# The modulation's product in a two-layer transformer kernel: split operands and four cheap products in place of one full-precision product

## What is computed

```python
# first block, layer 0: the NSA heads of the mixer (8 heads, 2 key groups, three branches)
pc = masked_softmax(q . kc)      # compressed keys: 31 columns
ps = masked_softmax(q . k_slc)   # selected keys, causal: up to 512 columns
pw = masked_softmax(q . k_win)   # window keys, causal: up to 512 columns
o  = g0 * pc @ vc + g1 * ps @ v_slc + g2 * pw @ v_win
# second block: the modulation, from two vectors c and c_ctx of 1024
sh1, sc1, g1, sh2, sc2, g2 = split(silu(c) @ ada_w + ada_b, 6)       # ada_w: 1024 x 6144
csh1, csc1, ...            = split(silu(c_ctx) @ ada_w + ada_b, 6)
```

## Time and profile before

| | |
|---|---|
| runs | 3551.23 us median of 3 (3548.71 to 3552.36) |
| the profiled execution | 3549.85 us, of which the span of the trace is 3548.4 us |
| PE busy | 3301.7 us, 93% |
| DVE busy | 2273.8 us, 64% |
| ACT busy | 1303.9 us, 37% |
| POOL busy | 807.3 us, 23% |
| granted TensorE clock, mean | 0.964 of full speed |

### The profile page before, as it was taken

One profiled execution on the slowest core, in us unless ns is written; L12 is line 12 of the kernel. 1 busy time (PEld: TensorE's weight loads), 2 busy tenths in 40 slices (PEclk: granted clock), 3 DMA queues, 4 the chain that ended last, 5 costly groups with the idle time before them and its releaser, 6 DMA issues. The chain is left out here.

```text
span 3548.4 us, 45109 instructions
## 1 busy us (share of the span) xinstructions
PE 3301.7 (93%) x17156; PEld 2753.9 (78%) x17156; DVE 2273.8 (64%) x4365; ACT 1303.9 (37%) x2284; POOL 807.3 (23%) x751
## 2 busy tenths in 40 slices
PE   7999989999999999997998998866889999999998
PEld 6445548888766688885776877766889999999998
DVE  4666445646455565464553336997778888888886
ACT  3333333223333332233453223225863333343433
POOL 1000341000100020004000002376853333334341
PEclk9999989999999999997998998988999999999999
DMA  3332102222211132222111222243579989899883
GB/s 136 125 108 76 51 24 89 95 102 87 93 48 42 42 107 91 100 89 69 65 35 57 90 89 83 85 159 129 211 274 316 323 309 321 308 319 316 308 313 124
DMA packets 180454, 515.17 MB, mean 145 GB/s; under 512 B 14992, under 2 KB 75408, under 8 KB 175120
## 3 DMA queue, kind: packets, MB, share of 16 engines
q1 hardware_dynamic: 128256, 305.70, 25.1%
q0 software_dynamic: 40464, 160.45, 13.2%
q10 hardware_dynamic: 11520, 46.15, 3.4%
HBM read 477.10 MB, written 35.13 MB: 144 GB/s over the span
## 5 line engine op out<-in xcount | busy, mean ns | idle before, releaser
L230 PE MATMUL bank<-h_hi,w_hi 128*128 128x512 f32 (+1 forms) x2528 | 970.4, 384 | 76.3 <-ACT w_hi L198 21.1
L230 PE MATMUL bank<-h_lo,w_hi 128*128 128x512 f32 (+1 forms) x2528 | 953.9, 377 | 0.0
L204 DVE TENSOR_TENSOR w_lo<-w_raw,w_hi 128x1024 fp32r<-128x1024 f32 (+1 forms) x468 | 599.8, 1282 | 333.5 <-ACT w_hi L198 327.6
L198 ACT ACTIVATE w_hi<-w_raw 128x1024 fp32r<-128x1024 f32 (+1 forms) x508 | 546.0, 1075 | 543.8 <-PE bank L230 526.3
L230 PEld LDWEIGHTS bank<-h_hi,w_hi 128*128 128x128 f32 x2528 | 487.9, 193 | 163.4 <-issue 48.5
L230 PE MATMUL bank<-h_hi,w_lo 128*128 128x512 f32 (+1 forms) x2528 | 596.7, 373 | 16.3 <-POOL w_lo L211 16.3
L230 PEld LDWEIGHTS bank<-h_lo,w_hi 128*128 128x128 f32 x2528 | 488.9, 193 | 67.4 <-issue 11.4
L230 PEld LDWEIGHTS bank<-h_hi,w_lo 128*128 128x128 f32 x2528 | 460.0, 189 | 86.1 <-POOL w_lo L211 17.6
L230 PE MATMUL bank<-e_hi,w_hi 128*128 128x384 f32 x1024 | 345.4, 337 | 5.9 <-DVE e_lo L2262 5.9
L230 PE MATMUL bank<-e_lo,w_hi 128*128 128x384 f32 x1024 | 344.2, 336 | 0.0
L2171 POOL DMA_INDIRECT own_row<-in_u_rows,own_e x128 | 157.9, 1233 | 321.5 <-DVE sums L2299 277.5
(11 more groups left out here) (405 smaller groups left out, 4754.1 us busy)
## 6 DMA issues: line engine op xcount, KB each, us to landing
w_raw<-in_w SPq DMA_DIRECT2D x476, 512.0 KB
ada_w<-in_ada_w POOLq DMA_DIRECT2D x24, 1024.0 KB, 5.1
expert_weights<-G ACTq DMA_DIRECT2D x12, 2048.0 KB, 7.3
Gin<-expert_weights SPq DMA_DIRECT2D x32, 768.0 KB
w_raw<-in_w SPq DMA_DIRECT2D x32, 704.0 KB
hidden_ahead<-u_stage ACTq DMA_DIRECT2D x40, 192.0 KB, 3.4
ahead<-hidden_ahead SPq DMA_DIRECT2D x20, 384.0 KB
na_bias<-in_bias ACTq DMA_DIRECT2D x4, 896.0 KB, 4.5
```

What stands on the lines that cost most here:

```text
L198: sc.activation(w_hi[s][:, 0:n], w_raw[raw_slot[u]][:, 0:n], ACT.Copy).then_inc(*w_hi_made.next(u))
L204: ve.tensor_tensor(w_lo[s][:, 0:n], w_raw[raw_slot[u]][:, 0:n], w_hi[s][:, 0:n], ALU.subtract).then_inc(*w_lo_made.next(u))
L230: m = te.matmul(out, wt, moving, start=(not low and k == 0 and moving is hi), stop=(low and k == len(blocks) - 1))
```

## The change

The modulation's product is taken apart as the large products are. DVE splits silu(c) once into a rounded part and a rest, side by side as `silu4` [128, 8, 4] of type fp32r. `ada_w` is loaded in halves of 512 KB into four buffers. For each half, ACT makes the rounded copy `ada_hi` (L807 of the new kernel) and POOL the rest `ada_lo` (L811); both lie in the tiles 0 to 3 of `o_hi` and `o_lo`, two buffers each. PE then does 4 matmuls with the four columns of `silu4` against `ada_hi` and 4 against `ada_lo` (L796, L799), where it did 4 fp32 matmuls with two columns. A row of the result is [4, 256], and the turn (L817) adds its two parts by a product with `fold` in place of the identity. ACT makes the copy for slot g+1 behind the exponentials of slot g; POOL makes the rest behind that, and then issues the load of four halves ahead. On PE the half product moves from ahead of the query matmuls and the value sums to behind them, to the end of the slot. The making of `fold` waits for the load of `ident`, one of the kernel's first.

```diff
-        ada_in = [loaded(f"ada_in{b}") for b in range(2)]
+        silu4 = sb(st, "silu_parts", [P, KT, 4], F32R)
+        fold = sb(st, "ada_fold", [4, 2])
+        ada_in = [loaded(f"ada_in{b}") for b in range(4)]
...
+        ada_hi, ada_lo = [[o[:, 2 * b:2 * b + 2, :].rearrange("p u (c n) -> p (u c) n", n=256) for b in range(2)] for o in (o_hi, o_lo)]
...
-            ve.tensor_tensor(silu[:, :, :], silu[:, :, :], col("c", 0, 16).rearrange("p (k c) -> p k c", c=2), ALU.mult).then_inc(*dve.next("silu"))
+            ve.tensor_tensor(silu[:, :, :], silu[:, :, :], col("c", 0, 16).rearrange("p (k c) -> p k c", c=2), ALU.mult).then_inc(*dve.next())
+            ve.wait_ge(*dve.here())
+            ve.tensor_copy(silu4[:, :, 0:2], silu[:, :, :]).then_inc(*dve.next())
+            ve.wait_ge(*dve.here())
+            ve.tensor_tensor(silu4[:, :, 2:4], silu[:, :, :], silu4[:, :, 0:2], ALU.subtract).then_inc(*dve.next())
+            ve.wait_ge(*ident_in.at("in"))
+            ve.tensor_tensor(fold[:, :], ident[0:4, 0:2], ident[0:4, 2:4], ALU.add).then_inc(*dve.next("silu"))
...
-            for c in range(4 * half, 4 * half + 4):
-                m = te.matmul(sums, silu[:, c, :], ada_w[k % 2][:, c, :], start=(c == 0), stop=(c == KT - 1))
+            te.wait_ge(*act.at("ada hi", g))
+            for c in range(4):
+                te.matmul(sums, silu4[:, 4 * half + c, :], ada_hi[g % 2][:, c, :], start=(half == 0 and c == 0), stop=False)
+            te.wait_ge(*pool.at("ada lo", g))
+            for c in range(4):
+                m = te.matmul(sums, silu4[:, 4 * half + c, :], ada_lo[g % 2][:, c, :], start=False, stop=(half == 1 and c == 3))
+            m.then_inc(*pe.next("ada", g))
+
+        def ada_scalar(g):
+            if g < slots:
+                sc.wait_ge(*ada_in[g % 4].at(g))
+                if g >= 2:
+                    sc.wait_ge(*pe.at("ada", g - 2))
+                sc.activation(ada_hi[g % 2], ada_w[g % 4][:, :, :], ACT.Copy).then_inc(*act.next("ada hi", g))
+
+        def ada_pool(g):
+            gp.wait_ge(*act.at("ada hi", g))
+            gp.tensor_tensor(ada_lo[g % 2], ada_w[g % 4][:, :, :], ada_hi[g % 2], ALU.subtract).then_inc(*pool.next("ada lo", g))
...
-                for n in range(2) if g == 1 else (g,) if 1 < g < slots else ():
-                    ada_tensor(n)
...
+                if g in (1, 2):
+                    ada_tensor(g - 1)
+                if g == 2:
+                    ada_turn(0)
+                if 2 <= g < slots:
+                    ada_tensor(g)
...
+                for n in range(2) if g == 0 else (g + 1,):
+                    ada_scalar(n)
...
+            for g in range(4):
+                ada_fetch(g)
+            for g in range(slots):
+                ada_pool(g)
+                gp.wait_ge(*pool.here())
+                ada_fetch(g + 4)
```

More of the change, by code:

```diff
@@ L632, in nsa @@
         Pm = [[[sb(st, f"nsa_p{hh}{m}{b}", [P, w]) for b, w in enumerate(widths)] for m in range(2)] for hh in range(2)]
-        ada_w = [sb(st, f"ada_w{b}", [P, KT, 256]) for b in range(2)]
-        rows_of = [sb(st, f"ada_rows{b}", [2, 256]) for b in range(2)]
+        ada_w = [sb(st, f"ada_w{b}", [P, 4, 256]) for b in range(4)]
+        rows_of = [sb(st, f"ada_rows{b}", [4, 256]) for b in range(2)]
+        ada_hi, ada_lo = [[o[:, 2 * b:2 * b + 2, :].rearrange("p u (c n) -> p (u c) n", n=256) for b in range(2)] for o in (o_hi, o_lo)]
         PT = [[sb(st, f"nsa_pt{hh}{b}", [P, (w + P - 1) // P, P]) for b, w in enumerate(widths)] for hh in range(2)]
@@ L780, in ada_tensor @@
             k, half = divmod(g, 2)
[L781 to L785, removed]
-            for c in range(4 * half, 4 * half + 4):
-                m = te.matmul(sums, silu[:, c, :], ada_w[k % 2][:, c, :], start=(c == 0), stop=(c == KT - 1))
-            if half:
-                m.then_inc(*pe.next("ada", k))
+            sums = lin[UQ[k // 6] % 2][0:4, 0:256]
+            if half == 0 and k % 6:
+                te.wait_ge(*dve.at("ada rows", k - 1))
+            te.wait_ge(*act.at("ada hi", g))
[14 more added lines that the diff above has]
+            gp.tensor_tensor(ada_lo[g % 2], ada_w[g % 4][:, :, :], ada_hi[g % 2], ALU.subtract).then_inc(*pool.next("ada lo", g))
         def ada_turn(k):
@@ L794, in ada_turn @@
             for n in range(2):
-                m = te.matmul(lin[UQ[k // 6] % 2][:, at + 2 * n:at + 2 * n + 2], rows_of[k % 2][:, n * P:(n + 1) * P], ident[0:2, 0:2], start=True, stop=True)
+                m = te.matmul(lin[UQ[k // 6] % 2][:, at + 2 * n:at + 2 * n + 2], rows_of[k % 2][:, n * P:(n + 1) * P], fold[:, :], start=True, stop=True)
             m.then_inc(*pe.next("ada turned", k))
         def ada_rows(k):
-            ve.wait_ge(*pe.at("ada", k))
+            ve.wait_ge(*pe.at("ada", 2 * k + 1))
             if k >= 2:
                 ve.wait_ge(*pe.at("ada turned", k - 2))
-            ve.tensor_copy(rows_of[k % 2][:, :], lin[UQ[k // 6] % 2][0:2, 0:256]).then_inc(*dve.next("ada rows", k))
+            ve.tensor_copy(rows_of[k % 2][:, :], lin[UQ[k // 6] % 2][0:4, 0:256]).then_inc(*dve.next("ada rows", k))
         def ada_vector(p):
@@ L845, in tensor @@
                         t.then_inc(*pe.next("nsa turned", hh, g - 3))
-                if 0 < g <= slots and g % 2 == 0:
+                if 2 < g <= slots and g % 2 == 0:
                     ada_turn(g // 2 - 1)
-                for n in range(2) if g == 1 else (g,) if 1 < g < slots else ():
-                    ada_tensor(n)
                 if g < slots and p < 3:
@@ L940, in gpsimd, with ada_fetch @@
             after(gp, "nsa projections")
[L941 to L944, removed]
+            def ada_fetch(g):
+                if g < slots:
+                    k, half = divmod(g, 2)
+                    gp.dma_start(ada_w[g % 4][:, :, :], io["ada_w"][k].rearrange("p k n -> p (k n)")[:, 1024 * half:1024 * half + 1024]).then_inc(*ada_in[g % 4].next(g))
+            for g in range(4):
[4 more added lines that the diff above has]
+                ada_fetch(g + 4)
         first_tensor()
```

## The result

The changed kernel took 3574.52 us (median of 4 runs, 3567.05 to 3578.78), the kernel before 3550.22: 1.0066 of its time, 95% interval 1.0048 to 1.0084. It is slower by 24 us where 24 us less were forecast. The profiled execution took 3578.78 us.

A forecast was written before the change was run, and what follows sets the result against it. PE was taken to bound the slots. Product -37.9, type changes +7.2, chain +4.6, value sums +3.5 and start -1.5 gave -24.1 us: 3527 us from a median of 3551.23, range 3516 to 3565.

The forecast's parts named there:

- What bounded the kernel: In the slots: PE's instructions set the time, busy 64.81 of 64.84 us in a block; the other engines have room.
- Product -37.9: PE's half products: eight fp32r matmuls take 1.10 us instead of 1.89, saving 37.9 us over 48 halves.
- change of type +7.2: PE, each slot: one more change to fp32r and back, 0.15 us a slot, +7.2 us (bounds 0 and +10.6).
- Chain +4.6: Exponentials, ACT's copy, POOL's subtraction, last four matmuls: this chain outlasts PE's work in short slot pairs, +4.6 us.
- Value sums +3.5: Value sums right behind the transposes wait for ACT's copy, 0.35 us each in some odd slots, +3.5 us.
- Start -1.5: Kernel start: the first half needs a smaller load, slot 3 begins earlier, -1.5 us (bounds -3 and +4).
- It costs little by itself: L593 and L595 held by POOL's subtraction: 0.5 to 0.9 us delay, on work PE wants three slots later.
- Rival 1: Every slot: POOL's subtraction holds DVE's L584, the exponentials wait; gain gone, +9 us to 3560 us; chance 0.30.
- Rival 2: Most slots: L584 free, but copy and subtraction late by 0.3 us; 14 us back, 3541 us; chance 0.14.
- Rival 3: PE's matmuls don't get cheaper, four weight columns taking as long as fp32 passes: 3551 + 15; chance 0.06 with the rest.
- The clock: At the start only: upper bound of +4 us if PE stays longer at half clock.

The follow-up runs named there:

- e1: Changed kernel without POOL's 48 subtractions, the second four matmuls taking the high part again (low part's product missing): 3531.1 us, ratio 0.9942.
- e8: Kernel before the change with only the product moved behind the value sums, no copy or subtraction, fp32 matmuls as before: 3561.73 us, ratio 1.0033.
- e12: e9 without its extra wait: POOL subtracts as soon as ACT's copy is there. 3565.09 us, ratio 1.0042.
- e4: Changed kernel with the modulation's 48 weight loads issued by SyncE instead of POOL, four next-stage loads moved ahead in its queue: 3573.25 us, ratio 1.007.
- e5: Changed kernel with one more wait: POOL's subtraction starts only after DVE has written the previous slot's probabilities. 3555.4 us, ratio 1.0016.
- e3: Changed kernel with the gate product at L593 written as a tensor_scalar instead of a two-input tensor_tensor: 3570.6 us, ratio 1.0054.
- e9: e5 with the product in the middle of the next slot, rows, turn and `mod` later, query pieces in slots 2 to 9: 3524.74 us, ratio 0.9931.

## Why the prediction was wrong

- **What bounded the kernel**: right. With PE's work cut, slots 13 to 23 of e1 got shorter by just that.
- **Product -37.9 and change of type +7.2**: 8.71 us in 11 slots is 0.79 us a slot, 37.9 for 48, with the changes between fp32r and fp32 in it. (The order adds nothing in these slots: they take 60.06 us in e8 and 60.04 in before.) The first term was right, the second should have been 0, its lower bound.
- **Chain +4.6**: PE waited 5.4 us for POOL in after. Size right.
- **Value sums +3.5**: PE's waits have no row for them after. 0.
- **Start -1.5**: slot 3 began 15.69 us behind slot 0 where it was 15.44: +0.3, within the bounds.
- **The order**: no term for it, and 11 us (e8). I costed each wait of PE in the new chain, but not what the product had covered in its old place, the turn to `mod` to first query piece.
- **The step that failed**: "It costs little by itself ... 0.5 to 0.9 us of delay falls on work that PE asks for three slots later." The 0.5 to 0.9 us are right for the first head (0.65 us in slot 12). Two things were missed. The delayed second gate meets a second subtraction, since nothing but ACT's copy keeps POOL from doing the next slot's in the same short slot; that one costs 2.5 us. And probabilities are indeed wanted three slots later, but masks, rows and `mod` stand behind the gate in DVE's queue and are wanted at once. Together with the half clock this is 43 us (after against e1).
- **Rival 1** had the sign and not the mechanism: L584 stayed at 154 ns. Rival 2's engines were the right ones, with 1.5 us lost on average at 23 of the 96 gates (2.5 us at ten of them) in place of 0.3 in most slots. Rival 3 is refuted by e1.
- **The clock**: the prediction had it only at the start. In the stage PE's idle time grew by 22 us and its busy time by 4, though its work at full clock fell by about 0.79 x 48 = 38. By this estimate some 40 us, the larger part of what was lost, came through the clock.

With the sum mended: -37.9 of product, +11 of order (e8) and +43 of subtractions beside DVE (after less e1) make +16; measured +24. The missing 8 us are in e1 already, with 27 us of half clock in its stage where e8 has 14; what brings them is open.

## What to carry to other kernels

An engine with room isn't free if it works beside one that it can hold: ask not only which instruction is held and for how long, but what stands behind it in its queue and how soon the bounding engine wants that. Tie such work to the phase in which it disturbs nothing (here one wait gave 19 us, and 40 once the order had slack), and when a piece of work is moved, look for the wait that it used to cover. If the bounding engine is TensorE, a short idle stretch can cost more than its length, as in e8 and e12.

## What the runs showed of the hardware

- A `tensor_tensor` of one element for a partition, 160 ns alone, takes up to 2.23 us when it begins inside POOL's 128x1024 subtraction (e4), and 2.68 to 2.86 when it begins inside a DMA issue of POOL with the subtraction right behind (after, e5). A `tensor_scalar` of one element was never held: with its scalar from another tile it stayed at 212 to 217 ns in all of 96, of which 15 began inside a subtraction (e3), and L584 at 153 to 156, of which 41 did (after). On 31, 128 and 256 elements it was held, up to 2.87 us.
- At 166.32 (after) the gate began 0.3 us ahead of the subtraction's record (166.62) and was held by it all the same. Every gate held by a subtraction that was recorded after the gate's own start had begun inside a DMA issue of POOL with the subtraction 0.02 us behind the issue, ten times in after and once in e5. Where 0.2 us or more lay between issue and subtraction, as at 158.14 in e5, no gate was held. Nor was one in e1, with 48 issues and no subtraction (no gate over 163 ns), and in e4, with no issue on POOL, none was held by a subtraction that had not begun. It doesn't always happen: two gates of after and three of e12 that began inside such an issue took 158 to 161 ns.
- Two idle stretches of PE of 1.84 us, in a stage otherwise at full clock, were each followed by 3.4 us at the lower of the two levels (e8); before, without them, the clock stayed up from 99.6 to 400 us. Which idle stretches lower it is not settled: e5 and e9 have 14.3 and 13.4 us of idle time in the stage, but 72 and 20 us at the lower level.
